# First eight modulation units: one float32 product in four column groups instead of a product split in high and low parts

## The reference, cut to what matters

```
mod   = silu(c) @ w_ada + b_ada            # (1, 6*1024)
mod_c = silu(c_ctx) @ w_ada + b_ada        # the same weights, for the context tokens
sh1, sc1, ... = split(mod, 6);  csh1, csc1, ... = split(mod_c, 6)
hl = rms_norm(x + pos, g_mix_pre) * (1 + sc1) + sh1          # 1024 latent tokens
hc = rms_norm(ctx, g_mix_pre) * (1 + csc1) + csh1            # 256 context tokens
...
p  = [hc; hl] @ w_in                       # the input projection, first its gate columns G
```

## Time and profile before

| | |
|---|---|
| time of three runs | 1339.75, 1340.05, 1342.15 us |
| span of the profiled execution | 1339.0 us |
| profiled execution's own time | not given apart from its span |
| busy: PE, DVE, ACT | 1265.4, 950.9, 776.2 us |
| G done (last matmul of L2209 in the chain) | 78.46 us from the start of the span |
| unit 10 there for ACT | 85.07 us |

### The profile page before, as it was taken

How to read it: one execution, slowest core, us unless ns; L and a number is a source line. 1 busy time by engine, 2 the same in 40 slices (tenths; PEclk the granted TensorE clock), 3 DMA queues, 4 the chain that set the end, 5 groups by cost and what they waited for, 6 DMA issues and landing times.

```text
span 1339.0 us, 18966 instructions
## 1 busy us (share of the span) xinstructions
PE 1265.4 (95%) x7151; PEld 1100.0 (82%) x7151; DVE 950.9 (71%) x1104; ACT 776.2 (58%) x911; POOL 119.1 (9%) x127
## 2 busy tenths in 40 slices
PE   6899999999999999999997599999999999999994
PEld 4888788898988999878886588888888888888883
DVE  5857431278666862584546988888888898888887
ACT  6643321374425454782333277777777777777785
POOL 1100000010000000041000111111111000111034
PEclk9999989999999999999998799999999999999997
DMA  9851160143454411304226599999999999999995
GB/s 376 280 119 34 62 189 0 48 127 111 158 221 172 174 65 33 142 22 184 79 80 230 228 362 352 406 400 405 397 396 396 396 391 399 397 396 396 395 312 211
DMA packets 77659, 319.35 MB, mean 239 GB/s; under 512 B 6568, under 2 KB 31176, under 8 KB 47832
## 3 DMA queue, kind: packets, MB, share of 16 engines
q1 hardware_dynamic: 70336, 290.14, 55.2%
q0 software_dynamic: 7264, 28.40, 8.5%
HBM read 291.15 MB, written 35.75 MB: 244 GB/s over the span
## 4 chain that ended last, share of the span: by engine, by line
PE 82%; DVE 9%; ACT 4%; DMA 3%; issue 1%; SPq 0%; POOLq 0%; POOL 0%; DVEq 0%; ACTq 0%
PE psum L2656 37%; PE psum L2263 7%; PE psum L2592 7%; PE psum L2321 3%; PE psum L2322 3%; PE psum L2323 3%; PE psum L2352 1%; PE psum L2353 1%; PE psum L2354 1%; DMA ada_raw<-w_ada_units 1%; PE psum L2164 1%; PE psum L2404 1%; PE psum L2679 1%; PE psum L2405 1%; PE psum L2673 1%
## 5 line engine op out<-in xcount | busy, mean ns | idle before, releaser
L2026 DVE TENSOR_TENSOR e_lo<-e_raw,e_hi 128x2048 fp32r<-128x2048 f32 x192 | 432.8, 2287 | 43.5 <-ACT e_hi L1331 43.5
L1331 ACT ACTIVATE e_hi<-e_raw 128x2048 fp32r<-128x2048 f32 x192 | 365.8, 1916 | 82.9 <-PE psum L2656 81.8
L2656 PE MATMUL psum<-e_hi,xt_hi 128*128 128x512 f32 x496 | 153.3, 390 | 0.1
L2656 PE MATMUL psum<-e_lo,xt_hi 128*128 128x512 f32 x496 | 152.9, 389 | 0.0
L2656 PE MATMUL psum<-e_hi,xt_lo 128*128 128x512 f32 x496 | 152.8, 389 | 0.0
L2656 PEld LDWEIGHTS psum<-e_hi,xt_lo 128*128 128x128 f32 x496 | 93.1, 188 | 19.6
L2656 PEld LDWEIGHTS psum<-e_lo,xt_hi 128*128 128x128 f32 x496 | 93.1, 188 | 19.6
L2656 PEld LDWEIGHTS psum<-e_hi,xt_hi 128*128 128x128 f32 x496 | 92.8, 188 | 19.8 <-DVE xt_lo L2030 0.5
L2321 PE MATMUL psum<-w_hi,h_hi 128*128 128x256 f32 x352 | 101.4, 288 | 0.0
L2322 PE MATMUL psum<-w_hi,h_lo 128*128 128x256 f32 x352 | 100.3, 285 | 0.0
L2323 PE MATMUL psum<-w_lo,h_hi 128*128 128x256 f32 x352 | 100.2, 285 | 0.0
(11 more groups left out here) (436 smaller groups left out, 2435.5 us busy)
## 6 DMA issues: line engine op xcount, KB each, us to landing
e_raw<-w_e_units SPq DMA_DIRECT2D x192, 1024.0 KB, 7.5
ada_x<-w_ada_units SPq DMA_DIRECT2D x16, 1024.0 KB, 4.8
raw<-w_in_units SPq DMA_DIRECT2D x13, 1024.0 KB, 6.8
ada_raw<-w_ada_units SPq DMA_DIRECT2D x8, 1024.0 KB, 21.9
bc<-rows_dram SPq DMA_DIRECT2D x16, 512.0 KB, 3.8
xs<-x SPq DMA_DIRECT2D x4, 1024.0 KB, 10.4
acc_dram<-zero_r SPq DMA_DIRECT2D x1, 4096.0 KB, 19.8
wo_raw<-w_out SPq DMA_DIRECT2D x4, 1024.0 KB, 6.0
```

The lines of the kernel that those rows point to most:

```text
L1331: act.activation(e_hi[u % EH][:], e_raw[u][:], ACT.Copy).then_inc(e_hi_ok, 1)
L2026: dve.tensor_tensor(e_lo[u][:], e_raw[u][:], e_hi[u % EH][:], ALU.subtract).then_inc(e_lo_ok, 1)
L2656: m = pe.matmul(o[:, BANK * b:BANK * (b + 1)], x[:, k, :], w[:, D * j + BANK * b:D * j + BANK * (b + 1)], start=a, stop=z)
```

## The change

All eight units are multiplied in one way, and unsplit. `c_z` holds each of the eight slices of the vectors in 32 columns, two of them used and the rest zero. `ada_to_rows` makes that slice stationary and streams 256 columns of the unit in float32; slice k writes to PSUM partitions 32(k mod 4) to 32(k mod 4)+31, so that slices 0 to 3 go to four different groups of columns of the array and slices 4 to 7 add to them. The four partial rows stand 32 partitions apart; `one_s` has ones at these places, so the step to columns adds them. The roundings and subtractions of the units, `c_st`, `c32` and the narrow matmuls are gone. DVE scales token block 6 as well, ACT only 7, 8 and 9, and the order on all three engines is written anew; the split of unit 9 moves behind the last token block.

```diff
+        c_z = at("c_z", AT_OUT + 58 * KB, [P, KC, 32])
-        c_st = at("c_st", AT_OUT + 58 * KB, [P, KC, P], F32R)
-        c32 = at("c32", AT_OUT + 62 * KB, [P, KC, 2])
...
         def ada_ps(i):
-            return psum[:, (4 + i % 2) * BANK:(4 + i % 2) * BANK + UW]
+            if i < 4:
+                return psum[:, (4 + i % 2) * BANK:(4 + i % 2) * BANK + UW]
+            return psum[:, 6 * BANK + UW:7 * BANK]
...
+            for g in range(4):
+                pool.wait_ge(konst, 9 + g)
+                pool.affine_select(out=v, in_=v, compare_op=ALU.not_equal, fill=1.0, base=-32 * g,
+                                   pattern=[[-1, 2]], channel_multiplier=1).then_inc(konst, 1)
...
             scale_tile(9)
-            ada_split_hi(0)
-            scale_tile(8)
-            scale_tile(7)
-            scale_tile(6)
-            ada_split_hi(1)
-            ada_split_hi(2)
+            ada_evac_rows(0)
+            for t in range(X_DVE, TA - 1):
+                scale_tile(t)
+            ada_evac_rows(1)
             x_mod(0)
...
-            ada_split_lo(0)
             mod_pair(0)
-            ada_split_lo(1)
-            ada_split_lo(2)
             x_hi(0)
             x_lo(0)
-            ada_split_lo(3)
-            ada_split_lo(4)
+            mod_pair(1)
             x_hi(1)
-            ada_split_lo(5)
-            mod_pair(1)
             x_lo(1)
             split_lo(8)
...
+            def ada_to_rows(i):
+
+                n = ADA_ORDER[i]
                 pe.wait_ge(ada_full[n], 16)
+                if i < 4:
+                    at_least(pe, ada_evac, i - 1)
+                elif i % 2 == 0:
+                    pe.wait_ge(mod1_ready, i // 2)
+                else:
+                    pe.wait_ge(ada_evac, i)
+                for k in range(KC):
+                    g = slice(32 * (k % 4), 32 * (k % 4 + 1))
+                    x = pe.matmul(ada_ps(i)[g, :], c_z[:, k, :], ada_raw[n][:, k, :], start=k < 4, stop=k >= 4)
+                x.then_inc(ada_rows, 1)
```

More of the change, by code:

```diff
@@ L96 @@
 ADA_ORDER = (0, 4, 1, 5, 2, 6, 3, 7)
-ADA_SPLIT = (1, 5, 2, 6, 3, 7)
-N_SPLIT = len(ADA_SPLIT)
+N_ADA = len(ADA_ORDER)
 X_FIRST = 6
+X_DVE = 7
 EU = 12
@@ L293, in split_count @@
         def split_count(n):
-            return n - 7 + N_SPLIT
+            return n - 7
         def acc_count(j):
@@ L885, in _ @@
             act.wait_ge(s_small, 16)
+            act.wait_ge(c_ready, 1)
             cc = col("c").rearrange("p (k r) -> p k r", k=KC)
-            act.activation(c32[:], cc, ACT.Silu).then_inc(c_silu, 1)
+            act.activation(c_z[:, :, 0:2], cc, ACT.Silu).then_inc(c_silu, 1)
             act.wait_ge(s_pos, 48)
@@ L890, in _ @@
             act.activation(pos_hi[rows, :], pos_r[rows, :], ACT.Copy).then_inc(c_silu, 1)
-            act.wait_ge(c_ready, 1)
             act.activation(rstd[:, 15:16], zero_r[:, 0:1], ACT.Sqrt)
@@ L913, in scale_tile @@
                 act.activation(xs[:, t, :], xs[:, t, :], ACT.Copy, scale=rstd[:, t:t + 1]).then_inc(scaled, 1)
[L915 to L920, removed]
             def ada_evac_rows(i):
@@ L924, in ada_evac_rows @@
                 if i >= 2:
-                    act.wait_ge(ada_cols, 2 + i - 1)
+                    act.wait_ge(ada_cols, i - 1)
                 act.activation(mod_rows[:, i % 2, :], ada_ps(i), ACT.Copy).then_inc(ada_evac, 1)
@@ L939, in _ @@
             scale_tile(9)
-            ada_split_hi(0)
-            scale_tile(8)
-            scale_tile(7)
-            scale_tile(6)
-            ada_split_hi(1)
-            ada_split_hi(2)
+            ada_evac_rows(0)
+            for t in range(X_DVE, TA - 1):
+                scale_tile(t)
+            ada_evac_rows(1)
             x_mod(0)
-            ada_split_hi(3)
-            ada_evac_rows(0)
-            ada_split_hi(4)
+            ada_evac_rows(2)
+            ada_evac_rows(3)
             x_mod(1)
-            ada_evac_rows(1)
-            ada_split_hi(5)
-            ada_evac_rows(2)
             split_hi(8)
-            ada_evac_rows(3)
-            act.wait_ge(ada_rows, 4)
-            split_hi(9)
[L958 to L963, removed]
+            ada_evac_rows(4)
+            x_mod(2)
+            ada_evac_rows(5)
+            x_mod(3)
+            x_mod(4)
+            ada_evac_rows(6)
+            x_mod(5)
+            ada_evac_rows(7)
+            x_mod(6)
+            x_mod(7)
+            split_hi(9)
             def conv_first(i, part, h, has_ctx):
@@ L1460, in split_lo @@
                 dve.tensor_tensor(lo if n in (V1 - 1, V1) else lo[:], from_[:], hi if n in (O0, V1 - 1, V1) else hi[:], ALU.subtract).then_inc(lo_ready, 1)
[L1463 to L1467, removed]
+            dve.memset(c_z[:], 0.0)
+            dve.memset(zero_r[:], 0.0).then_inc(c_ready, 1)
             dve.wait_ge(c_silu, 2)
@@ L1498, in _ @@
                 scale_tile(t)
[L1499 to L1502, removed]
+            dve.wait_ge(mean_ready, 1)
+            for t in range(X_FIRST, X_DVE):
+                scale_tile(t)
             def mod_pair(q):
@@ L1538, in _ @@
             x_lo(2)
+            mod_pair(2)
             x_hi(3)
-            mod_pair(2)
             x_lo(3)
-            split_lo(9)
             x_hi(4)
             x_lo(4)
-            x_hi(5)
             mod_pair(3)
-            x_lo(5)
-            for k in range(6, KC):
+            for k in range(5, KC):
                 x_hi(k)
                 x_lo(k)
+            split_lo(9)
             link(dve.memset(row_b[:], 0.0))
@@ L1944, in aff_copy @@
                 v = lambda w: w.rearrange("p (q n) -> p q n", q=4)[:, s, :]
-                dve.wait_ge(aff_mm, after)
+                dve.wait_ge(aff_mm, N_ADA + after)
                 return dve.tensor_copy(v(left[0][0:2 * N_EXP, :]), v(psum[0:2 * N_EXP, 0:HALF]))
@@ L1963, in _ @@
                 if t == TL - 1:
-                    aff_copy(slice(1, 3), N_SPLIT + 1)
+                    aff_copy(slice(1, 3), 1)
                 if t + 2 < TL:
@@ L1987, in of_round @@
                 return left[r // 4][q:q + 2 * N_EXP, :], vals[q:q + 2 * N_EXP, r // 4, :]
-            aff_copy(slice(0, 4, 3), N_SPLIT + 2).then_inc(topk, 1)
+            aff_copy(slice(0, 4, 3), 2).then_inc(topk, 1)
             for r in range(ROUNDS):
@@ L2008, in by_half @@
                 return v[:, ::-1, :] if h else v
-            dve.wait_ge(sel_mm, N_SPLIT + 1)
+            dve.wait_ge(sel_mm, N_ADA + 1)
             v1, t1, lead, diff = (merge[:, j, :, :] for j in range(4))
@@ L2155, in unit_ready @@
                 pe.wait_ge(lo_ready, split_count(n))
-            def ada_unit(n):
-                a, q = n // 4, n % 4
+            def ada_to_rows(i):
+                n = ADA_ORDER[i]
                 pe.wait_ge(ada_full[n], 16)
[L2161 to L2171, removed]
+                if i < 4:
[4 more added lines that the diff above has]
+                    pe.wait_ge(ada_evac, i)
                 for k in range(KC):
-                    pe.matmul(ada_ps(i), c_st[:, k, :], hi[:, k, :], start=k == 0, stop=False)
-                for k in range(KC):
-                    x = pe.matmul(ada_ps(i), c_st[:, k, :], lo[:, k, :], start=False, stop=k == KC - 1)
+                    g = slice(32 * (k % 4), 32 * (k % 4 + 1))
+                    x = pe.matmul(ada_ps(i)[g, :], c_z[:, k, :], ada_raw[n][:, k, :], start=k < 4, stop=k >= 4)
                 x.then_inc(ada_rows, 1)
             def ada_to_cols(i):
-                a, q = ADA_SPLIT[i] // 4, ADA_SPLIT[i] % 4
-                pe.wait_ge(ada_evac, i + 1)
-                pe.wait_ge(mod1_ready, q)
+                a, q = ADA_ORDER[i] // 4, ADA_ORDER[i] % 4
+                pe.wait_ge(ada_evac, i + 1 if i < 4 else 2 * q + 2)
+                at_least(pe, mod1_ready, q)
                 for j in range(2):
@@ L2210, in g_ctx @@
                 i.then_inc(tile_mm, 2)
-            pe.wait_ge(konst, 11)
+            pe.wait_ge(konst, 13)
             pe.wait_ge(grid_ok, 2)
@@ L2221, in _ @@
                           start=False, stop=True).then_inc(pos_mm, 1)
-            ada_unit(0)
-            ada_unit(4)
             ada_to_rows(0)
+            ada_to_rows(1)
+            ada_to_cols(0)
+            ada_to_cols(1)
             pe.wait_ge(scaled, TA)
             x_block(0)
-            ada_to_rows(1)
+            ada_to_rows(2)
+            ada_to_rows(3)
             x_block(1)
[L2229 to L2235, removed]
             ada_to_cols(2)
             ada_to_cols(3)
+            x_block(2)
+            ada_to_rows(4)
             x_block(3)
-            x_block(4)
+            ada_to_rows(5)
             unit_ready(8)
-            pe.wait_ge(ada_evac, N_SPLIT)
+            pe.wait_ge(ada_evac, 4)
             g_lat(0)
-            x_block(5)
-            g_lat(1)
             ada_to_cols(4)
             ada_to_cols(5)
+            x_block(4)
+            g_lat(1)
+            ada_to_rows(6)
+            x_block(5)
+            ada_to_rows(7)
```

(4 more changed lines are left out.)

8 lines of the change are left out of this document (removed).

## The result

The changed kernel took 1329.24 us (median of four runs, 1327.73 to 1332.51), the kernel before beside it 1341.1 us (1339.75 to 1343.67): a ratio of 0.9914, with a 95% interval from 0.9894 to 0.9935. A second measurement of the same kernel later gave 1331.0 and 0.9927 (0.9914 to 0.9941).

What follows compares the result with a forecast made beforehand. The chain of waits to G's end at 78.46 us was taken as the bound. G 12.0 us earlier, less 0.5 for unit 10's longer load, gave 11.5: 1340.05 - 11.5 = 1328.5 us, range 1322 to 1336.

Steps and rivals of the forecast that it cites:

- The bound: First 80 us: a gapless chain of waits to G's last matmul at 78.46 us; gains there count at the end.
- The start: Unit 0 to block 0's transposes: these end at 30.6 instead of 39.4 us, 8.8 us ahead.
- The walk: Step-by-step timing from unit 0's landing to G's end after the change: 66.5 us, 12.0 us earlier than 78.46.
- The price of a unit: PE's unsplit product of one unit over four column groups: 1.27 us, or 2.54 at the low clock.
- The clock: PE before G's end: rises from the 1.2 GHz level at 36 us, with 31 and 41 us as ends.
- Unit 10's load: Load behind G, amid POOL's transfers: 0.5 us longer than 6.57; ends 1.9 shorter and 3.8 longer.
- rival 5: Behind G: POOL's queue holds unit 10 up by the full 3.8 us, 1332 us; 0.12 together with turning costs.
- What followed as a block: Everything behind unit 10 moves together, so 11.5 us gained there shortens the span from 1339.0 to 1327.5.
- rival 1: Units on PE: column groups do not overlap, 3.44 us a unit, G's end about 83.7, 1345 us; chance 0.09.
- Rival 2: Units on PE: groups overlap half, 1.72 us a unit, G's end at 69.9, 1332 us; chance 0.1.
- Rival 3: PE's twelve shape changes around units: turning costs three times 1.3 us, 2.6 more, 1331; 0.12 together with unit 10 held up.

Runs made afterwards that it cites:

- the run with 22 products: Changed kernel plus 22 float32 products of the identity with itself, filling PE's idle time before unit 0: 1329.07 us, ratio 0.9922.
- that kernel with the gates first: Kernel before, with ACT computing the gates' rows before rounding unit 10 and DVE subtracting for it after the gates' sums: 1339.88 us, ratio 0.9978.
- the other order: Changed kernel with each unit's eight slices issued as 0, 4, 1, 5, 2, 6, 3, 7: 1329.74 us, ratio 0.9917.
- holding POOL back: Changed kernel with POOL's two position transfers waiting until unit 10 has landed: 1323.74 us, ratio 0.9872.

## Why the prediction was right, and where not

The forecast was 1328.5 us, 11.5 us less than before; it came out 11.9 less than the kernel before measured beside it, by the path that the prediction describes. Point by point:

- **The bound.** That all before G's end counts held: 11.2 us of it passed through unit 10 to DVE's first row (82.13 here, 93.35 before) and on.
- **The start.** The end of block 0's transposes, forecast at 30.6, is 30.66 in the chain. The walk went by ACT's scalings, rightly; what it didn't say is that these wait for the input, so that, the narrow units gone, the chain starts there and not with unit 0.
- **The price of a unit.** I took 1.27 us, two thirds of a full overlap, from L2513. It is 1.00; that row was a poor neighbour, since row halves gave 1.35 of 2 and column groups give 3.57 of 4 (1.93 of 2); why the row halves overlap less no run shows. The Trainium skill's figure (TensorE: Matmul & The Clock Gate, section Measured speedup vs the span model: 2.38 times for three groups) was nearer, with an estimate of 1.09 for four.
- **The clock.** Taken up at 36 us; by the durations (3.57 for the two units to 34.23, then 1.04 for transposes) it rose at about 34. With both figures corrected the walk gives 64.2 for G, measured 64.81: the 66.5 was 1.7 too late.
- **Unit 10's load.** I took 0.5 us longer than 6.57, and it was 2.44. The mechanism (POOL's queue fills the engines) and both ends were in the text, the value was chosen too near the old one. By the prediction's own sign, over 9 us from G's end to unit 10's rounding, rival 5 came true, if barely (9.04 us). This mis-sized term and the two above offset one another: 12.0 - 0.5 foreseen, 13.65 - 2.4 measured. That they cancel to 0.3 us is luck; the sum is better than its parts.
- **What followed as a block** did so within 0.5 us (11.2 at the first row, 10.7 at the end). I had not seen that PE, no longer held by G, would wait 4.3 instead of 3.0 us ahead of unit 11 and run longer at the low clock behind it. It starts unit 11 11.2 us earlier (128.38, before 139.61), and by the starts of its matmuls the low clock costs 2.2 us there, against 1.6 before: an estimate, and about the 0.5 us that is missing at the end.
- **Rivals.** With one group the unit was 3.57 us and G at 83.4 (forecast 83.7), so rival 1 was priced rightly at G; its 1345 would have been 1340, as unit 10's load was shorter. Rival 2's 1.72 is what two groups give (1.85). Rival 3 is out: behind a unit the next eight transposes or six matmuls are 0.1 to 0.2 us longer than elsewhere (1.02 against 0.87 to 0.93; 1.59 against 1.39) with four groups and with one, about the 0.21 us of the earlier trace rows. Rival 5 was two thirds true: 2.4 of its 3.8 us.

## What to carry to other kernels

A float32 product with few output rows can go unsplit if its slices of the contraction are spread over the four column groups of PE and the four partial rows are added by a matmul that is needed anyway: 16 records take 1.00 instead of 3.57 us, and two engines lose the work of splitting. When a stage ends earlier, look at what else uses the queues at the new time, and at what stands in program order behind the transfer that it releases: here moving an unneeded rounding behind the gates' chain was worth another 0.5% (0.2% in the kernel before). Before shortening one input of a join, look at the other: ahead of the first transposes it is now the input that decides in all six profiles with four groups and no filling, and in the first of them unit 0 had 1.5 us to spare.

## What the runs showed that I had not expected

The landing of the loads varies: DVE's first addition started between 10.77 and 13.49 us in the profiles of the changed kernel and its variants. Unit 0 moves with it, from 20.90 to 23.63 us, so it is the whole stream of loads that shifts, and the kernel before is exposed to it as well (21.16 and 22.72 in its two profiles here). In the five profiles in which all up to the end of G was the same but for the order within a unit, that end followed the first addition to within about 0.5 us: an uncertainty of 2.7 us that no edit here touches.

A wait of PE can cost more than its length, and by how much is not settled by its length alone. Behind the wait of 4.3 us the clock was low, behind that of 1.2 us it was not; but it was low soon after a wait of 1.4 us in the run with 22 products, and of two waits of 3.1 us at the same place, in the kernel before and in that kernel with the gates first, only the second was followed by the low level. In the comparison with the other order, holding POOL back gained 6.0 us from a load that was 4.4 us shorter.
